# Nineteen stage-closing barriers without GpSimd's drain, in a one-core kernel for two transformer blocks

## The reference: what is computed

```
first_block:  h = rms_norm(x) @ w_in            -> pool part, q, k, v
              x = x + concat(multiscale_pool, diff_attention(q, k, v)) @ w_out
              x = x + cross_attention(rms_norm(x), rms_norm(mem))         # 256 memory rows, 4 heads
              x = x + moe_ffn(rms_norm(x))      # 32 experts, top 4, w_gu 1024x2048, w_down 1024x1024
second_block: p = modulate(rms_norm(x)) @ w_in
              y_a = rwkv7_mix(...)              # a recurrence over 512 steps, 12 heads
              y_b = dilated_attention_mix(...)  # windows 128/512/2048, dilation 1/4/16
              x = x + gate * rms_norm((sigmoid(ga)*y_a + sigmoid(gb)*y_b) @ w_out)
              x = x + gate * rms_norm((silu(u) * g) @ w_ffn_out)
```

## Time and profile before

| what | value |
|---|---|
| time, median of 3 runs | 2658.79 us (2658.34 to 2662.72) |
| the profiled execution's own time | 2658.82 us |
| its span (first to last instruction) | 2657.0 us |
| what lies around the span | 1.8 us |
| PE busy | 2476.0 us, 93% |
| DVE busy | 1071.3 us, 40% |
| ACT busy | 659.1 us, 25% |
| POOL busy | 198.1 us, 7% |
| granted TensorE clock, mean | 0.971 of full speed |

### The profile page before, as it was taken

One profiled execution on the slowest core, in us unless ns is written; L12 is line 12 of the kernel. 1 busy time (PEld: TensorE's weight loads), 2 busy tenths in 40 slices (PEclk: granted clock), 3 DMA queues, 4 the chain that ended last, 5 costly groups with the idle time before them and its releaser, 6 DMA issues. The chain is left out here.

```text
span 2657.0 us, 55525 instructions
## 1 busy us (share of the span) xinstructions
PE 2476.0 (93%) x24050; PEld 1564.5 (59%) x24050; DVE 1071.3 (40%) x1767; ACT 659.1 (25%) x1179; POOL 198.1 (7%) x174
## 2 busy tenths in 40 slices
PE   7989987999999999999999799789788799899998
PEld 6658855333344443433334478467677677788887
DVE  5584444322233323332222344557555434422233
ACT  4253331000000000000000332456454223422222
POOL 0002000100000000010000200001221000000000
PEclk9989998999999999999999899999999899999999
DMA  5253312999999999999999832520101223122220
GB/s 204 98 189 125 113 34 108 411 415 416 417 416 417 417 417 417 417 417 417 417 416 417 321 119 83 182 83 32 45 4 47 111 91 127 60 99 95 95 95 32
DMA packets 125173, 586.96 MB, mean 221 GB/s; under 512 B 15824, under 2 KB 29776, under 8 KB 80400
## 3 DMA queue, kind: packets, MB, share of 16 engines
q1 hardware_dynamic: 99952, 539.07, 51.3%
q10 hardware_dynamic: 18176, 24.98, 2.7%
q0 software_dynamic: 6912, 20.98, 2.1%
HBM read 564.00 MB, written 20.97 MB: 220 GB/s over the span
## 5 line engine op out<-in xcount | busy, mean ns | idle before, releaser
L1258 PE MATMUL psum<-weight_ring,expert_xT 128*32 128x512 f32 x3120 | 343.7, 595 | 7.4 <-DVE expert_xT L1339 6.7
L368 DVE TENSOR_TENSOR w_low<-weight_ring,w_high 128x2048 fp32r<-128x2048 f32 (+1 forms) x92 | 213.5, 2321 | 320.8 <-ACT w_high L363 320.4
L1258 PE MATMUL psum<-more_weights,expert_xT 128*32 128x512 f32 x3024 | 338.3, 596 | 3.4 <-DVE expert_xT L1339 3.4
L1258 PEld LDWEIGHTS psum<-weight_ring,expert_xT 128*32 128x32 f32 x3120 | 101.1, 110 | 235.8 <-issue 224.3
L363 ACT CAST w_high<-weight_ring 128x2048 fp32r<-128x2048 f32 (+1 forms) x88 | 166.6, 1893 | 289.7 <-PE psum L402 143.8
L1258 PEld LDWEIGHTS psum<-more_weights,expert_xT 128*32 128x32 f32 x3024 | 96.5, 110 | 199.9 <-issue 192.9
L1347 DVE TENSOR_TENSOR gate<-psum,bias_rows 128x768 f32<-128x768 f32 x32 | 30.6, 957 | 439.9 <-PE psum L1258 439.9
L1274 PE MATMUL psum<-more_weights,expert_hT 128*32 128x256 f32 x3168 | 176.9, 379 | 1.5 <-DVE expert_hT L1369 1.5
L1218 POOL DMA_INDIRECT expert_x<-hidden,index x96 | 98.5, 1026 | 1047.9 <-DVE index L1328 845.2
L1274 PE MATMUL psum<-weight_ring,expert_hT 128*32 128x256 f32 x2976 | 166.3, 379 | 0.0
L402 PE MATMUL psum<-mix_hT_high,w_high 128*128 128x512 f32 x384 | 155.9, 406 | 6.5 <-PEq L1940 3.5
(11 more groups left out here) (540 smaller groups left out, 3997.8 us busy)
## 6 DMA issues: line engine op xcount, KB each, us to landing
weight_ring<-in_w_gu SPq DMA_DIRECT2D x130, 1024.0 KB, 21.0
more_weights<-in_w_gu SPq DMA_DIRECT2D x126, 1024.0 KB, 19.3
more_weights<-in_w_down SPq DMA_DIRECT2D x66, 1024.0 KB, 22.4
weight_ring<-in_w_down SPq DMA_DIRECT2D x62, 1024.0 KB, 23.1
weight_ring<-in_w_in SPq DMA_DIRECT2D x35, 1024.0 KB, 6.6
weight_ring<-in_w_ada SPq DMA_DIRECT2D x24, 1024.0 KB, 4.8
weight_ring<-in_w_ffn_in SPq DMA_DIRECT2D x22, 1024.0 KB, 4.8
expert_table<-expert_y ACTq DMA_DIRECT2D x128, 96.0 KB, 7.9
```

The costliest lines, as they stand in the source:

```text
L368: self.m.nc.vector.tensor_tensor(low, w, high.bitcast(F32), ALU.subtract).then_inc(self.ready.sem, 1)
L1258: ins = T.matmul(ps[j][part(q), :], xT[:, j, k, :], w[:, :, q, :], start=(k == 0), stop=(k == GUN - 1))
```

## The change

```diff
@@ first_norm, and 18 more blocks in the same way @@
-    with nc.Block() as block:
+    with nc.Block(no_gpsimd_drain=True) as block:
@@ SplitBiases.split @@
         pool.wait_ge(step.sem, step.at(5))
-        Q.tensor_copy(bias[q, :], full[q, :])
-        loaded.end(48), step.end(5)
+        Q.tensor_copy(bias[q, :], full[q, :]).then_inc(step.sem, 1)
+        pool.wait_ge(step.sem, step.at(6))
+        loaded.end(48), step.end(6)
```

## The result

The changed kernel takes 2674.61 us (median of 7 runs), the kernel before in the same set of runs 2663.14 us. The ratio is 1.0042, 95% interval 1.0029 to 1.0056: slower by 11.5 us, between 7.7 and 14.9. In a second set of runs the ratio was 1.0042 again (1.0027 to 1.0058). The forecast was 2660.2 us and "within 0.2%": too low, and 0.2% lies outside the measured interval.

A forecast was written before the change was run, and what follows sets the result against it. PE, busy 93% of the span, was taken as the bound on average, with barriers stopping every engine. Span 2657.0 + 1.4 (signals) = 2658.4 us, plus 1.8 around it: 2660.2 us, +0.05%; range 2657.9 to 2663.4 us.

The forecast's parts named there:

- Removing the 18 drains: 0 us.: All 18 barriers: POOL's drains end at least 10.0 us before their barrier, so removing them saves 0 us.
- POOL's row in L3871 stays at 34 ns.: Closing block: sign expected in the changed profile, POOL's remaining drain unchanged at 34 ns.
- Rival C: Closing block in `finish`: draining is only put off and paid there, at most 14.4 us, 2674.6 us; chance 0.05.
- The argument against C: L1452 and L1190: gathers land 6.0 us after issue, explaining L1452's drain and leaving 4.2 us unexplained in L1190.
- a smaller form of C: Closing block: a put-off drain price of only 4 us, 2664 us; half of the 0.05 chance.
- A semaphore instruction more in each barrier: All 18 barriers: the last engine's separate signal adds 0.08 us each, 1.4 us in all; chance 0.90.
- The write with its own signal: POOL's cast at L1098: added signal and wait cost about 0.07 us, hidden 25 us before the barrier; 0 us.
- Rival B: First gathers of `moe_exit` and experts: slow starts come from earlier drains; removal saves 2.4 us, 2657.8 us; chance 0.04.
- I am wrong if a stage between two barriers changes its length by a microsecond or more.: Stages between barriers: a change of a microsecond or more in length was to refute the forecast.
- Rival D: Built program: the drains could still be there, time 2658.8 us; chance 0.01.
- The range: Whole kernel: forecast time between 2657.9 and 2663.4 us, with scatter of a median from the runs before.

The follow-up runs named there:

- no drain at all: Changed kernel with the no-drain flag also in the closing block, so POOL never drains after the program's start; ratio to the kernel before 1.0009, median 2664.33 us.
- explicit drains: Changed kernel with a POOL drain written out at the end of POOL's list in each of the 18 stages; ratio to the kernel before 0.9999, median 2663.16 us.

## Why the prediction was wrong, point by point

- **"Removing the 18 drains: 0 us."** The step that failed. That none of the 18 lay on the path was right, the covers of 10 to 67 us included. But the step took a drain for a wait, which is free when one comes late enough, and put what its removal leaves behind at nothing. Two of the 18 settled a bill that goes by the count of DMAs, 96 and 16, and without them all 112 were left to the closing block's drain: 9.2 us, with 0.4 us of cover, so 8.8 us on the path.
- **"POOL's row in L3871 stays at 34 ns."** Wrong: 9216 ns. Its 34 ns in the earlier trace rows were not a property of that place, but of an engine that had issued no DMA since its last drain. All 13 drains of 34 to 53 ns in empty stages said the same.
- **Rival C** had the mechanism, the place and the threshold, and I gave it 0.05. Its price of 14.4 us was too high: it added all that lay between the last gather's end and the end of the drain in L1190 and L1452, 9.2 and 5.5 us, and of these 5.3 and 4.8 us are the landing of the last gather. Measured were 112 x 0.0817 + 0.064 = 9.2 us, of which 8.8 exposed. That its 2674.6 us agrees with the measured 2674.61 is luck: a price 5.6 us too high was added to a first median that was 4.4 us below the one measured beside the changed kernel, and the 1.4 us by which the medians exceed the trace's two terms made up the rest.
- **The argument against C** was badly weighed. In L1452 the drain ended 0.4 us after the estimated landing (0.7 by the record of that gather), and I read "it waited for the transfer and for little else"; but behind 16 DMAs no more than 0.7 us is to be seen after a landing. In L1190 4.2 us were left (4.0 by the record), and six times as many gathers stood behind it. That was the one row that spoke of a price by count, and I kept it as "a smaller form of C" with half of 0.05. The two rows together give 4.6 us for 112. The full 9.2 could not be read from them, since both drains had a landing to wait for.
- **A semaphore instruction more in each barrier**, 0.08 x 18 = 1.4 us: held. Measured 0.066 x 18 = 1.19 us, and 0.08 of the first barrier's gap, as forecast (0.29 to 0.37). The four links of 0.29 us and the ACT instruction in the chain were the right rows, though 0.06 of the 0.29 lay before the end of DVE's drain: the four links took 0.24, 0.06 each. The Trainium skill's 44 ns a hop ("Runtime: NRT & Kernel Launch", section "The ~15µs preamble/postamble breakdown") gave 0.8 us. The trace doesn't agree, with its 1.19: what is added isn't a hop, which was there before, but the 48 ns before DVE's signal and its 21 ns (L583 above).
- **The write with its own signal**, 0 us: held. POOL's cast at L1098 ended at 268.0 us in the changed kernel and the barrier was at 293.6 us.
- **Rival B** (POOL's gathers start slowly because of an earlier drain): fell. The first gather of the experts took 2.39 us after the change as before, with no drain since the program's start.
- **"I am wrong if a stage between two barriers changes its length by a microsecond or more."** A poor sign: two stages changed by 4.1 and 5.5 us with the clock, and a kernel with the same barrier there has the second at its old length.
- **Rival D** (the drains still there) fell with the profile after, in which L583 and the others have no POOLq DRAIN.
- **The range** of 2657.9 to 2663.4 us was too narrow for another reason too. It took the scatter from three runs that spanned 4.4 us; the kernel before alone later gave medians up to 2663.14. With its upper end 4.4 us higher the range would still have missed 2674.61, so this was not the step that failed.

## What to carry to other kernels

When an operation that finishes something is removed, ask not only whether anybody waited for it, but which later one of its kind inherits what it did; look for the last one left, and what covers that. For GpSimd's drain: keep one behind the last of its DMAs, in a stage where GpSimd is idle, and the one at the end of the program is all but free (34 to 46 ns). The same kind of instruction at 34 ns in one place and 13 us in another, with more work behind it, is a question to settle before giving a chance of 5%.

## What the runs showed of the hardware

- POOL's drain costs 0.064 us plus 0.0817 us for each DMA that POOL issued since its last drain (9 points from 3 to 112), the last of them landed some 7 us to over 1100 us earlier. Behind gathers still under way it ends 0.041 us plus 0.0409 us for each after the last has landed (5 counts from 15 to 112), half of that. With no DMA since the last drain it takes 34 to 53 ns. 16 indirect gathers gave 1361 ns, 16 plain copies 1357 ns. The same count gave the same number in different kernels and places: 5281 ns twice for 64, and 9216 ns three times and 9207 ns once for 112.
- A barrier in which the last engine signals with its drain takes 0.063 to 0.068 us less than one with a separate signal behind a bare drain: 2.98 us over 18 barriers, against 4.17, 4.20 and 4.12 in the three kernels whose 18 barriers all have the new form (changed, no drain at all, explicit drains).
- A drain that POOL leaves out is not made up for at the program's end: 1.8 us lay around the span with a drain of 9.2 us in it, with one of 34 ns, and with none.
